# Corner gates from one stacked block, shorter sample dot products, another order at the begin, and the last norm's roots by token

## The reference

```python
def layer(x, ...):
    h = rmsnorm(x, norm_mix)
    q, k, v, g_ret, x_lru, y_lru, g_a, g_b = split(h @ w_in)
    ...                                   # retention in 4 heads with rope; a group norm; @ w_ret_out
    xc, new_buf = causal_conv(x_lru, conv_buf, conv_w, conv_b)
    # RG-LRU: 1280 channels in 16 blocks of 80, block-diagonal gate maps
    r = sigmoid(einsum('blnc,ncd->blnd', xb, w_a) + b_a)
    i = sigmoid(einsum('blnc,ncd->blnd', xb, w_x) + b_x)
    log_a = -8 * r * softplus(-lam)
    ...                                   # scan over the tokens
    lru_branch = (gelu(y_lru) * hl) @ w_lru_out
    merged = sigmoid(g_a + b_gate[0]) * ret_branch + sigmoid(g_b + b_gate[1]) * lru_branch
    x = x + merged @ w_o
    gt, up = split(rmsnorm(x, norm_ffn) @ w_gate_up)
    return x + (silu(gt) * up) @ w_down

y = rmsnorm(x, norm_final)                # after both layers: x * rsqrt(mean(x*x) + eps) * g
```

## Time and profile before

| | us |
|---|---|
| median of 3 runs (2431.92 to 2433.31) | 2432.12 |
| the profiled execution | 2431.23 |
| its span in the profile | 2429.4 |
| TensorE matmuls busy | 2395.8 (99%) |
| GpSimd busy | 1727.2 (71%) |
| VectorE busy | 1204.4 (50%) |
| ScalarE busy | 630.7 (26%) |

### The profile page before, as it was taken

How to read it: one execution, slowest core, us unless ns; L and a number is a source line. 1 busy time by engine, 2 the same in 40 slices (tenths; PEclk the granted TensorE clock), 3 DMA queues, 4 the chain that set the end, 5 groups by cost and what they waited for, 6 DMA issues and landing times.

```text
span 2429.4 us, 51213 instructions
## 1 busy us (share of the span) xinstructions
PE 2395.8 (99%) x19460; PEld 2345.1 (97%) x19460; DVE 1204.4 (50%) x1610; ACT 630.7 (26%) x913; POOL 1727.2 (71%) x1970
## 2 busy tenths in 40 slices
PE   7999999999999999999999999999999999999997
PEld 7999999999999999999999999999999999999997
DVE  7665555577754522022366554545786544221222
ACT  2312121326751210011113222221466412100110
POOL 7474757588887777777865756565888877777774
PEclk9999999999999999999999999999999999999998
DMA  5554545322233222322235635453222322223222
GB/s 176 183 187 158 183 155 188 142 96 85 88 100 92 92 92 85 100 86 87 94 130 204 225 140 187 151 183 106 91 92 83 98 97 91 92 84 101 87 86 88
DMA packets 113001, 296.76 MB, mean 122 GB/s; under 512 B 11680, under 2 KB 12448, under 8 KB 112864
## 3 DMA queue, kind: packets, MB, share of 16 engines
q1 hardware_dynamic: 60480, 198.21, 24.9%
q10 hardware_dynamic: 52384, 96.56, 11.4%
HBM read 254.34 MB, written 40.38 MB: 121 GB/s over the span
## 4 chain that ended last, share of the span: by engine, by line
PE 68%; DVE 2%; ACT 1%; DVEq 1%; issue 0%; POOL 0%; ACTq 0%; POOLq 0%
PE banks L395 63%; PE banks L562 1%; PE banks L570 1%; PE banks L531 1%; PE banks L586 1%; PE banks L548 0%; DVE scratch L1095 0%; POOL w_low L381 0%; PE banks L484 0%; DVE ret_acc L1338 0%; DVE scratch L1157 0%; PE banks L442 0%; DVEq L1092 0%; DVE scratch L842 0%; PE banks L540 0%
## 5 line engine op out<-in xcount | busy, mean ns | idle before, releaser
L381 POOL TENSOR_TENSOR w_low<-w_raw,w_high 128x256 fp32r<-128x256 f32 (+1 forms) x1544 | 1285.1, 862 | 61.7
L376 POOL TENSOR_SCALAR w_high<-w_raw 128x1024 fp32r<-128x1024 f32 (+3 forms) x420 | 439.2, 1046 | 619.0 <-PE banks L395 578.0
L395 PE MATMUL banks<-x_high,w_high 128*128 128x260 f32 x4096 | 831.3, 284 | 16.0 <-DVE x_low L749 11.0
L395 PE MATMUL banks<-x_high,w_low 128*128 128x260 f32 x4096 | 825.5, 283 | 0.0
L395 PE MATMUL banks<-x_low,w_high 128*128 128x260 f32 x4096 | 823.5, 283 | 0.0
L395 PEld LDWEIGHTS banks<-x_high,w_high 128*128 128x128 f32 x4096 | 632.2, 189 | 24.5 <-issue 17.0
L395 PEld LDWEIGHTS banks<-x_high,w_low 128*128 128x128 f32 x4096 | 631.3, 188 | 0.0
L395 PEld LDWEIGHTS banks<-x_low,w_high 128*128 128x128 f32 x4096 | 631.0, 188 | 0.0
L395 PE MATMUL banks<-split_scratch,w_high 128*128 128x260 f32 x3776 | 606.9, 282 | 2.1 <-POOL w_low L381 0.9
L395 PEld LDWEIGHTS banks<-split_scratch,w_high 128*128 128x128 f32 x3776 | 517.1, 188 | 3.6 <-ACT split_scratch L1613 1.3
L395 PE MATMUL banks<-split_scratch,w_low 128*128 128x260 f32 x1888 | 380.0, 283 | 0.0
(11 more groups left out here) (170 smaller groups left out, 1926.5 us busy)
## 6 DMA issues: line engine op xcount, KB each, us to landing
w_raw<-in_wstream SPq DMA_DIRECT2D x268, 512.0 KB, 3.5
w_raw<-in_wstream SPq DMA_DIRECT2D x88, 384.0 KB, 3.0
scratch<-in_sret ACTq DMA_DIRECT2D x64, 512.0 KB, 6.8
out_ret_s<-scratch ACTq DMA_DIRECT2D x64, 512.0 KB, 3.5
scratch<-v_rows ACTq DMA_DIRECT2D x64, 256.0 KB, 4.1
w_raw<-in_wstream SPq DMA_DIRECT2D x48, 320.0 KB, 2.8
w_raw<-in_wstream SPq DMA_DIRECT2D x16, 448.0 KB, 3.2
out_ret_p<-scratch ACTq DMA_DIRECT2D x8, 512.0 KB, 2.8
```

The source lines that it names most:

```text
L376: pool.tensor_scalar(WH[:, j, w], WR[:, j, w], 1.0, 0.0, ALU.mult, ALU.add)
L381: m = pool.tensor_tensor(WL[:, j, p], WR[:, j, p], WH[:, j, p].bitcast(F32), ALU.subtract)
L395: m = pe.matmul(out, wt[:, w, blk * P:(blk + 1) * P], x[xi], start=first and n == 0, stop=last and n == 2)
```

## The change

Four edits.

1. *Corners.* For t = 0 and t = 4 the neighbour's part is at most 32 channels deep (CR = 32). The second block of an outer gate tile holds those 32 weight rows three times. GpSimd makes WH and WL of it as for any block and then copies rows 64 to 95 of WL over those of WH. ScalarE's new `corner(g, t)` fills XS: the 32 rows of XCH, of XCL and of XCH again. One matmul of 96 rows for each half then gives all three passes. A corner's gate tile takes 6 + 2 matmuls.
2. *Sample dot products.* VectorE multiplies q by k and adds the two halves, so QKW is one block, and TensorE sums it with one matmul.
3. *Begin.* ScalarE loads its table ahead of the norm weights, and issues x tiles 4 to 7 between the copies. The first two tiles of layer 0 take each other's places in PSUM (FIRST_Q), so that tile 3 waits for tile 0's read alone.
4. *Last norm.* The last residual's square is not added. TensorE sums SSQ and that square by token (the tokens on partitions, one column each for 4 + 1 token blocks); roots and reciprocals are taken of 128 x 4 and 8 x 1 values; VectorE multiplies the identity by them into diagonal blocks DG, and TensorE multiplies ONES by those, which puts the inverse roots of all tokens on every partition of a PSUM tile. The 8 output tiles read them from PSUM.

```diff
+CR = 32
+OUTER = (0, GT - 1)
+CORNER_UNITS = {B_Y[g][t] + 1 for g in range(GROUPS) for t in OUTER}
+CORNER_BLOCKS = [MT + 2 * w + 1 - YG_UNIT[0] for w in range(2)]
...
+        XS = R[:, (2 * GT + 4) * TOK:(2 * GT + 5) * TOK]
...
                                     m = pool.tensor_tensor(WL[:, j, p], WR[:, j, p], WH[:, j, p].bitcast(F32),
                                                            ALU.subtract)
+                                for b in CORNER_BLOCKS if base + k in CORNER_UNITS else ():
+                                    if b0 <= b < b1:
+                                        pool.drain()
+                                        c = slice(b * P, (b + 1) * P)
+                                        pool.tensor_copy(WH[2 * CR:3 * CR, j, c], WL[2 * CR:3 * CR, j, c])
+                                        m = pool.drain()
                                 m.then_inc(s["w_split"], 1)
...
                     for i in range(3, QK + VT):
-                        whole(ub, i, tb, i, XH, XL)
+                        if first and layer == 0 and i == 3:
+                            pe.wait_ge(s["t_free"], tb + 1)
+                            whole(ub, i, tb, i, XH, XL, place=FIRST_Q[0])
+                        else:
+                            whole(ub, i, tb, i, XH, XL)
...
                             pe.wait_ge(s["qk_wide"], hh + 1)
-                            for d in range(KT):
-                                pe.matmul(AUX[:, BANK[N_SC + j], P:P + 1], QKW[:, d, :], ONES[:, 0:1],
-                                          start=d == 0, stop=d == KT - 1)
+                            pe.matmul(AUX[:, BANK[N_SC + j], P:P + 1], QKW[:, 0, :], ONES[:, 0:1],
+                                      start=True, stop=True)
...
-                    else:
-                        pe.wait_ge(s["xc_low"], layer * LT + (g * GT + BAND[t][-1] + 1))
-                        xs = [pairs(XCH, XCL, k) for k in BAND[t]]
+                        for w in range(2):
+                            q = spread(ub0, u, YG_UNIT[t], tb0, idx + 1 + w, xs, q)
+                        return
+                    pe.wait_ge(s["xc_low"], layer * LT + (g * GT + t + 1))
+                    pe.wait_ge(s["xs_full"], layer * (GROUPS * len(OUTER)) + (g * len(OUTER) + OUTER.index(t) + 1))
                     for w in range(2):
-                        q = spread(ub0, u, YG_UNIT[t], tb0, idx + 1 + w, xs, q)
+                        tile_begin(tb0, idx + 1 + w)
+                        outs = [PP[:, slot(idx + 1 + w), c, 0:HALF] for c in range(2)]
+                        b = CORNER_BLOCKS[w]
+                        product(outs, ub0, u + 1, b - 1, pairs(XCH, XCL, t), True, False)
+                        for c in range(2):
+                            m = pe.matmul(outs[c], WH[0:3 * CR, (u + 1) % 2, b * P:(b + 1) * P],
+                                          XS[0:3 * CR, c * HALF:(c + 1) * HALF], start=False, stop=True)
+                        m.then_inc(s["p_done"], 1)
...
-            norm_sums(2 * DEPTH)
+            def token_sums(src, start):
+                for i in range(TT + 1):
+                    t = slice(i * P, min((i + 1) * P, TOK))
+                    m = pe.matmul(token_sum(i)[0:t.stop - t.start], src[:, t], ONES[:, 0:1],
+                                  start=start, stop=not start)
+                return m
+
+            pe.wait_ge(s["x_sum"], MT * (2 * DEPTH + 1) - 1)
+            token_sums(SSQ, True)
+            pe.wait_ge(s["x_sq"], MT * (2 * DEPTH + 1))
+            token_sums(SQT[:, 1, :], False).then_inc(s["sq_mm"], 1)
+            for i in range(TT + 1):
+                pe.wait_ge(s["r_diag"], i + 1)
...
+                        m = pe.matmul(PP[:, S_WIDE, c, a - c * HALF:b - c * HALF], ONES[0:n, :],
+                                      DG[0:n, a:b], start=True, stop=True)
...
-                    tt(wide(QKW[:]), samples(QF), KSC[:].rearrange("p d (j r) -> p d j r", r=ROUNDS),
-                       ALU.mult).then_inc(s["qk_wide"], 1)
+                    tt(QKP[:], QF[:, :, SEQ:TOK], KSC[:], ALU.mult)
+                    dve.drain()
+                    part = QKP[:].rearrange("p d (j r) -> p d j r", r=ROUNDS)
+                    tt(wide(QKW[:]), part[:, 0:1], part[:, 1:2], ALU.add).then_inc(s["qk_wide"], 1)
...
-            root_inverse(RINV[:])
+            dve.reciprocal(RS[:, 0:TT], RS[:, 0:TT])
+            dve.reciprocal(RS[0:NS, TT:TT + 1], RS[0:NS, TT:TT + 1])
             dve.drain()
+            for i in range(TT + 1):
+                n = min(P, TOK - i * P)
+                ts(DG[0:n, i * P:i * P + n], ID[0:n, 0:n], RS[0:n, i:i + 1], None, ALU.mult
+                   ).then_inc(s["r_diag"], 1)
+            dve.wait_ge(s["r_wide"], 1)
...
             load_x(0)
-            act.dma_start(NRM[:], norms).then_inc(s["norm_ld"], 16)
-            for m in range(1, MT):
-                load_x(m)
             act.wait_ge(s["boot"], 1)
             A(TOUCH, EPST, ACT.Sqrt)
+            act.dma_start(NRM[:], norms).then_inc(s["norm_ld"], 16)
+            X_AHEAD = 4
+            for m in range(1, X_AHEAD):
+                load_x(m)
             act.wait_ge(s["norm_ld"], 16)
...
+                def corner(g, t):
+
+                    n = g * len(OUTER) + OUTER.index(t)
+                    before = C_RET + MT if n == 0 else C_Y[(n - 1) // 2][OUTER[(n - 1) % 2]] + 3
+                    act.wait_ge(s["p_done"], tb0 + before)
+                    b, r = (t + 1, slice(0, CR)) if t == 0 else (t - 1, slice(P - CR, P))
+                    act.wait_ge(s["xc_low"], layer * LT + (g * GT + b + 1))
+                    A(XS[0:CR, :], XCH[r, b, :], copy)
+                    A(XS[CR:2 * CR, :], XCL[r, b, :], copy)
+                    A(XS[2 * CR:3 * CR, :], XCH[r, b, :], copy).then_inc(s["xs_full"], 1)
+
...
                 for t in range(GT):
                     conv_high(0, t)
+                    if t == GT - 2:
+                        corner(0, 0)
...
                         neighbours(0, 1)
                         neighbours(0, 2)
+                        corner(0, GT - 1)
                     sig_ga(t)
                     if t == 1:
                         neighbours(0, 3)
+                corner(1, 0)
                 neighbours(1, 1)
                 conv_high(1, GT - 1)
                 gated_high(GT - 1)
...
                 neighbours(1, 2)
+                corner(1, GT - 1)
                 gated_high(GT)
...
-            norm_root(2 * DEPTH + 1)
+            act.wait_ge(s["sq_mm"], 2 * DEPTH + 1)
+            A(RS[:, 0:TT], AUX[:, :, 0], ACT.Sqrt, bias=EPST, scale=1.0 / DM)
+            A(RS[0:NS, TT:TT + 1], token_sum(TT)[0:NS], ACT.Sqrt, bias=EPST[0:NS], scale=1.0 / DM
+              ).then_inc(s["x_sd"], 1)
```

62 lines of the change are left out of this document (46 added, 16 removed).

## The result

The changed kernel takes 2442.07 us (median of 6 runs, 2440.61 to 2443.34) against 2431.91 for the one before (6 runs, 2431.64 to 2433.31): ratio 1.0041, 95% interval 1.0031 to 1.0051. It is slower by 10.2 us, where 4.0 were forecast; 2442.07 lies 0.6 above the range. The profiled execution took 2441.88 (span 2440.1, 10.7 more than before).

A forecast was written before the change was run, and what follows sets the result against it. The prediction took TensorE as the bound, its matmuls busy 2395.8 of 2429.4 us. Terms +8.1 - 1.8 - 0.3 - 2.0 = +4.0 us gave a median of 2436.1, range 2427.5 to 2441.5.

The forecast's parts named there:

- the three places: TensorE waits: gate-A read about 1.0 us, first gates of group 1 4 to 5, lru_out(1) some 4.
- The corners on ScalarE ... +8.1 us: Recurrent stages: three copies a corner at 0.65 us delay TensorE by 4.07 a layer, net of part of the saving.
- 0.92 of margin: Gate-A tile read behind corner(0,4): VectorE starts 1.95 us later with 0.92 to spare, so TensorE waits about 1.0.
- Nothing stays: First gate of group 0: corner(0,0) delays it about 0.6 us, taken up by the 0.54 wait for neighbour copies.
- The corners on GpSimd ... no time on the path.: Corner units: copies and drains take 1.2 us a unit, covered; without that cover 9.6 us.
- The rival that had this mechanism: GpSimd ends last in corner units: +9.6 us in series gives 2445.7, half of it 2441; chance 0.08.
- The corners on TensorE ... 7.7 us: Corner gate tiles: 16 tiles lose 4 matmuls each at 0.121 us, 7.7 us, if 96-row passes cost like 128.
- an all-hidden case: Recurrent stages: ScalarE's copies all fall in idle time, -11.8 us in all, 2420.3; chance 0.12.
- Halved sample products, -1.8: Sample dot products in heads: four one-column matmuls become two, 16 x 0.11 us saved; VectorE's extra add is covered.
- The begin, -0.3: Kernel start: early table load counted as 0, tile 3 earlier but tile 4 held by VectorE; bounds -1.6 to +1.5 us.
- The end, -2.0: Last norm: small roots and reciprocals replace the 3.40 us reciprocal, first output earlier; -1.2 to -3.0 us.
- The 96-row pass as another shape: Corner gates: a shape switch of 1.03 us once for each of 16 gates, +16.5, 2452.6; chance 0.05.

The follow-up runs named there:

- kernel 3: The change without GpSimd's copies of the low rows and their drains; 2440.52 us, ratio 1.0035 to the kernel before.
- kernel 1: The change without its corner edit: sample products, begin and end alone; 2428.67 us, ratio 0.9983 to the kernel before.
- kernel 2: kernel 1 plus ScalarE's corner copies at the change's places and TensorE's wait for them, 12 matmuls a corner gate tile; 2441.24 us.
- kernel 9: kernel 2 with ScalarE's corner copies moved to the places where ScalarE idles, as in kernel 5; 2428.44 us.
- kernel 10: kernel 1 plus GpSimd's copies and drains alone, 12 matmuls a corner gate tile, no ScalarE copies; 2432.72 us.
- kernel 5: The whole change with each corner's three ScalarE copies moved to places where ScalarE had idled; 2437.90 us.
- Kernel 8: The change without any corner copies on ScalarE or GpSimd, keeping 6 + 2 matmuls a corner gate tile; 2427.68 us.
- kernel 4: The change with one of corner(0,4)'s three copies moved ahead of the third root; 2439.92 to 2443.63 us, ratio 1.0044.
- kernel 6: kernel 5 with GpSimd's corner work made one copy of 32x256 and two drains in the unit's second half; 2433.52 us.

## Why the prediction was wrong, step by step

**The sign and the three places were right, the size was not**: +4.0 forecast, +10.2 measured. Two terms failed, and the runs give each its number. The corners with their copies on ScalarE stood in the sum with +8.1; kernel 3, which adds just these to kernel 1, has +12.0. GpSimd's copies stood there with nothing; the change lies 1.6 above kernel 3. The other three edits stood there with -4.1; kernel 1 has -3.7. 12.0 + 1.6 - 3.7 = 9.9.

By tile starts of the profiled execution against before, net of the matmuls saved at each place, a stage loses:

| us | layer 0 | layer 1 |
|---|---|---|
| corner(0,0), to x(1,1) | 0.4 | 0.5 |
| the wait ahead of x(1,2) | 2.1 | 2.1 |
| the half clock in that tile | 1.6 | 1.6 |
| from there to y(1,0), behind corner(0,4) | 0.7 | 1.0 |
| the first gates of group 1 and ga(5) | 0.6 | 0.5 |
| lru_out(1) | 1.3 | 1.3 |
| the rest | -0.2 | 0.1 |

The forecast had 1.0 at x(1,2), 4.57 in all by lru_out(1), and -0.5 behind it. By its own terms:

*"The corners on ScalarE ... +8.1 us"*: the term was too small. The copies cost 0.65 each, as the row said (1834.77, 1835.40, 1836.05 in the change), and TensorE waits at the three places that were named. What failed is the slack. The 0.92 of margin was taken against 1.95 alone; VectorE's ring also became 1.05 longer, because its operations met GpSimd's at other moments. The step had no term for the clock: 1.5 us a layer at the x tile in the change. And "Nothing stays" of corner(0,0) was wrong, by the 0.4 and 0.5 above. Against these, the waits behind were smaller than forecast, since TensorE came late itself. That the copies are the price of their place and not of their amount is shown by kernels 2 and 9.

*"The corners on GpSimd ... no time on the path."* This step failed outright. The reasons given were 27 us of idle in the stage, work a unit ahead, and ScalarE's delays. The idle is a mean of the whole stage. At the turn of the groups GpSimd runs back to back, and by its two buffers it cannot use earlier idle time: it begins a unit when TensorE begins the one before. Alone the copies cost 4.2 us (kernel 10). The rival that had this mechanism got 0.08 and a price of 9.6 in series; with ScalarE out of the way 10.2 were measured. That the two are so near is luck: the 9.6 had neither the lost cover nor the half clock, which took 4.2 us in the profiled execution of kernel 5.

*"The corners on TensorE ... 7.7 us"* with -7.7 as what an all-hidden case would give. It would not. Kernel 8 hides everything, by leaving it out, and gets 0.8. The matmuls that were removed had been the cover under which GpSimd splits the next unit. I had written that the saved matmuls "only make the wait longer", but for ScalarE's reasons, and did not see that they would be lost without any copies too. So the case that I gave 0.12 and 2420.3 was not open at all. Of the last corner's saving the sum counted 0.5 a layer; in the change 0.2 stayed to the merge tiles.

*Halved sample products, -1.8*: two loads at 69.56 in the change, the next row at 69.78, 0.22 for two, so 0.11 each as in the earlier trace rows, and 16 x 0.11 stands. *The begin, -0.3*: tile 3 starts at 33.39 instead of 34.57 and tile 4 then waits 1.33 for VectorE's L954, the trade that was forecast; with 4 x 0.22 of sample products in the 0.68 gained by the first stage, about +0.2 is left for the begin. *The end, -2.0*: 8.25 - 6.12 = 2.1 in the change's trace. In kernel 1 the same edit gave 0.8 in one profiled execution and 1.6 in another, since the twelve passes ran at the lower clock there; kernel 1's total shows that the three edits save 3.7 together, against 4.1 forecast.

*The 96-row pass as another shape*: the two passes of a corner stand 0.12 from their neighbours, so that rival, given 0.05, is out:

```profile
1837.34 0.41 PE L425 MATMUL banks<-split_scratch,w_low 128*128 128x260 f32 x2
1837.58 0.40 PE L687 MATMUL banks<-split_scratch,w_high 96*128 96x260 f32 x2
1837.82 0.65 PE L425 MATMUL banks<-split_scratch,w_high 128*128 128x260 f32 x4
```

The Trainium skill, TensorEngine Tiling (Array Packing), section Tiling Modes, lists tilings of 128, 64 and 32 rows and none of 96. In this trace the pass pays no switch.

**What stays open.** Why the clock fell behind 2.10 us of idle in the change and not behind 2.12 and 2.13 in kernels 2, 3 and 4; the executions of kernel 5 differ by it among themselves, and no run here isolates a cause. And how the 2 us divide that are left of kernel 6's 5.0 beside the half clock: GpSimd's single copy was not tried without the saving.

## What to carry to other kernels

Before counting work removed from the bound engine as gain, look at who uses that work as cover: here 1 us less in a unit was 1 us more of waiting for the unit behind it, because another engine prepares units two buffers ahead and has its own time for each. Put helper copies where their engine waits for something anyway; the same twelve copies cost 12.7 us or nothing. And when two additions sit on two engines, run each alone and with the saving, since the later of two delays stays unseen until the first is gone.

## What the runs showed of the hardware

Copies of 32 partitions by 520 took 0.62 to 0.64 us on ScalarE, as those of 64 and of 128. Small VectorE operations of 8 to 11 columns (L1159 and L1164 of the change) took 0.16 to 0.17 us by themselves and 0.60 to 0.72 where they lay wholly beside GpSimd's subtractions. GpSimd's copy of 32x128 took 0.28 to 0.68 us, 0.57 in the middle. Behind waits of TensorE of 2.1 to 2.4 us the granted clock fell to its lower level in the change and in kernel 6, which cost 1.5 to 1.7 us each time; behind waits of 2.12 and 2.13 in kernels 2, 3 and 4 it did not.
